# Added quarters of a Strassen product formed in DRAM by accumulating transfers

## The reference

```
o_a, sfa, sba = gdn_branch(qkv, z_a, gate_cols, p, s_af, s_ab)
o_b, sfb, sbb = lru_branch(x_b, z_b, p, s_bf, s_bb, col_major)
pa = o_a @ p['w_proj_a']
pb = o_b @ p['w_proj_b']
g_a, g_b = jnp.split(jax.nn.sigmoid(h @ p['w_gate'] + p['b_gate']), 2, axis=-1)
mixed = (g_a * pa + g_b * pb) @ p['w_out']
return x + gate * mixed, sfa, sba, sfb, sbb
```

## Time and profile before

| | |
|---|---|
| median of 3 runs | 1506.69 us |
| profiled execution | 1505.08 us |
| its span | 1503.2 us |
| PE busy | 1463.1 us, 97% |
| DVE, ACT, POOL busy | 77%, 57%, 32% |
| granted clock, mean | 0.993 |
| DMA queue of SP | 142.12 MB, 30.3% of the 16 engines |

### The profile page before, as it was taken

How to read it: one execution, slowest core, us unless ns; L and a number is a source line. 1 busy time by engine, 2 the same in 40 slices (tenths; PEclk the granted TensorE clock), 3 DMA queues, 4 the chain that set the end, 5 groups by cost and what they waited for, 6 DMA issues and landing times. The chain is left out here.

```text
span 1503.2 us, 29073 instructions
## 1 busy us (share of the span) xinstructions
PE 1463.1 (97%) x11568; PEld 1401.1 (93%) x11568; DVE 1156.2 (77%) x1943; ACT 850.3 (57%) x1789; POOL 478.8 (32%) x376
## 2 busy tenths in 40 slices
PE   8999999999999999999999999999999998897997
PEld 7899999999999999999899999999999898897886
DVE  5789898988889898988847663663666689889864
ACT  6675847576675847575496376376376543443211
POOL 2122323222322323222212221221221686877420
PEclk9999999999999999999999999999999999999999
DMA  9422121222213131323212112112114747436242
GB/s 314 115 71 87 33 90 37 59 69 59 78 35 106 33 97 30 101 73 124 68 52 81 58 51 81 58 51 81 58 51 154 209 139 219 145 122 208 88 154 99
DMA packets 158409, 144.31 MB, mean 96 GB/s; under 512 B 7897, under 2 KB 139842, under 8 KB 158274
## 3 DMA queue, kind: packets, MB, share of 16 engines
q1 hardware_dynamic: 157986, 142.12, 30.3%
q10 hardware_dynamic: 288, 0.33, 0.1%
HBM read 122.34 MB, written 20.09 MB: 95 GB/s over the span
## 5 line engine op out<-in xcount | busy, mean ns | idle before, releaser
L139 PE MATMUL db<-h_hi,w_hi 128*128 128x384 f32 x816 | 288.0, 353 | 0.2 <-DVE w_lo L1477 0.2
L141 PE MATMUL db<-h_hi,w_lo 128*128 128x384 f32 x816 | 274.6, 336 | 0.0
L140 PE MATMUL db<-h_lo,w_hi 128*128 128x384 f32 x816 | 274.6, 336 | 0.0
L140 PE MATMUL mb<-h_lo,w_hi 128*128 128x384 f32 x696 | 233.9, 336 | 0.0
L139 PE MATMUL mb<-h_hi,w_hi 128*128 128x384 f32 x696 | 233.9, 336 | 0.0
L141 PE MATMUL mb<-h_hi,w_lo 128*128 128x384 f32 x696 | 233.9, 336 | 0.0
L2145 POOL TENSOR_TENSOR w_lo<-w,w_hi 128x1024 fp32r<-128x1024 f32 x29 | 81.3, 2805 | 314.3 <-ACT w_hi L2195 314.3
L2443 PE MATMUL mb<-h_hi,w_hi 128*128 128x288 f32 x448 | 138.3, 309 | 22.7 <-POOL w_lo L2156 22.3
L139 PEld LDWEIGHTS db<-h_hi,w_hi 128*128 128x128 f32 x816 | 153.7, 188 | 3.9 <-DVE w_lo L1477 0.7
L140 PEld LDWEIGHTS db<-h_lo,w_hi 128*128 128x128 f32 x816 | 153.9, 189 | 0.0
L141 PEld LDWEIGHTS db<-h_hi,w_lo 128*128 128x128 f32 x816 | 153.4, 188 | 0.0
(11 more groups left out here) (374 smaller groups left out, 3499.3 us busy)
## 6 DMA issues: line engine op xcount, KB each, us to landing
w<-in_w_in SPq DMA_DIRECT2D x48, 512.0 KB, 4.1
d_dt<-decay_rows SPq DMA_DIRECT2D x16, 576.0 KB, 6.6
d_qg<-decay_rows SPq DMA_DIRECT2D x16, 512.0 KB, 4.2
w<-in_w_gate SPq DMA_DIRECT2D x16, 512.0 KB, 4.2
w<-in_w_proj_a SPq DMA_DIRECT2D x24, 256.0 KB, 3.8
m_w<-in_w_proj_a SPq DMA_DIRECT2D x24, 256.0 KB, 3.4
w<-in_w_proj_b SPq DMA_DIRECT2D x24, 256.0 KB, 3.3
m_w<-in_w_proj_b SPq DMA_DIRECT2D x24, 256.0 KB, 3.2
```

The costliest lines, as they stand in the source:

```text
L139: pe.matmul(out, hi, rhi, start=(k == 0), stop=False)
L140: pe.matmul(out, hi, rlo, start=False, stop=False)
L141: return pe.matmul(out, lo, rhi, start=False, stop=(last and stop))
```

## The change

Two new DRAM arrays hold added quarters: `weight_sums` (four sums of 512 x 512 for each branch) and `row_sums` (three sums of 512 x 576 for each branch). Each is made by two transfers from DRAM to DRAM that POOL issues: the first copies one quarter, the second adds another one to it (`accum_op`). Since such a transfer can only add here, the signs of the scheme are chosen so that seven of the ten two-quarter operands are sums; product 6 takes its rows with the sign turned as they are split, and the results of products 1 and 6 are copied and added with other signs.

The weights' sums are formed during the eight heads of the front stage: in head h, POOL issues the adding transfer of sum h-1 and the copying one of sum h behind the low half of that head's second tile. Branch a's row sums follow behind low halves 4 and 8 of the 29 tiles, branch b's behind feeds 4 and 12 of the Strassen stage (about turns 3 and 11). Left to POOL and DVE in the stage are the weight sum of product 1 (phases 1 and 8) and the row sums of products 4 and 3 (phases 4, 5, 11, 12).

Rows are now loaded for each phase by itself, 14 loads in place of 8 (`QUAD` says into which of the four places), each when the low halves of the phase before in that place are done (`quads_in`). Rows are split one turn later than before: part_high(w+7) and part_low(w+6). The transposition of the branch b states in PE's list moves from turn 2 to turn 3.

```diff
+W_SUMS = ((5, (0, 0), (0, 1)), (7, (0, 1), (1, 1)), (2, (1, 0), (1, 1)), (6, (1, 0), (0, 0)))
+R_SUMS = ((1, (0, 0), (1, 1)), (7, (1, 0), (1, 1)), (6, (0, 0), (0, 1)))
+def row_sum(pool, W, src, br, at, second):
+    j, l = R_SUMS[at][1 + second]
+    part = src[j * KH * P:(j + 1) * KH * P, l * TH:(l + 1) * TH]
+    if second:
+        pool.dma_start(W.rsums[br, at], part, accum_op=ALU.add).then_inc(W.sems["dram_sums"], 16)
+    else:
+        pool.dma_start(W.rsums[br, at], part).then_inc(W.sems["dram_sums"], 16)
...
                 low(block_of(h, 1))
+                if h:
+                    pool.wait_ge(S["dram_sums"], 16 * (2 * h - 1))
+                    weight_sum(pool, A, W, h - 1, 1)
+                weight_sum(pool, A, W, h, 0)
                 pool.wait_ge(S["bf"], (h + 1) * Q)
...
-        COPIES = {5: ((0, 1, 1.0), (0, 0, -1.0)), 1: ((1, 1, 1.0),), 2: ((1, 0, 1.0),)}
+        COPIES = {5: ((0, 1, 1.0), (0, 0, -1.0)), 1: ((1, 1, -1.0),), 2: ((1, 0, 1.0),)}
...
+        QUAD = (0, 1, 2, 1, 2, 3, 1, 2, 0, 3, 1, 0, 3, 1)
+        WITH = {4: 1, 5: 0, 11: 1, 12: 2}
...
+                if m in R_SUM:
+                    sp.wait_ge(S["dram_sums"], 16 * (28 if br else 22))
+                    part = W.rsums[br, R_SUM[m]]
...
+            def quads_in(after, ns):
+                sp.wait_ge(S["r_lo"], was["r_lo"] + KH * (after + 1))
+                for n in ns:
+                    quad_in(n)
...
+                if m in W_SUM:
+                    sp.dma_start(raw_of(n)[:, 0:KH, :], W.wsums[br, W_SUM[m]].rearrange("(k p) n -> p k n", p=P)[
+                        :, :, p * P:(p + 1) * P]).then_inc(S[raw_sem(n)], 16)
+                    return
...
+                if n == 8:
+                    quads_in(1, (3,))
+                elif n == 12:
+                    quads_in(2, (4,))
+                elif n == 20:
+                    quads_in(4, (6, 7))
+                elif n == 24:
+                    quads_in(5, (8, 9))
...
+                if n == 4:
+                    pool.wait_ge(S["dram_sums"], 16 * 22)
+                    pool.wait_ge(S["store"], was["store"] + 16 * H)
+                    for at in range(len(R_SUMS)):
+                        row_sum(pool, W, ob, 1, at, 0)
+                elif n == 12:
+                    pool.wait_ge(S["dram_sums"], 16 * 25)
+                    for at in range(len(R_SUMS)):
+                        row_sum(pool, W, ob, 1, at, 1)
...
-                if w + 2 * KH < NPH * KH:
-                    part_high(w + 2 * KH)
+                if w + 2 * KH <= NPH * KH:
+                    part_high(w + 2 * KH - 1)
```

More of the change, by code:

```diff
@@ L1957, in tail_stage @@
         part_sums = lambda n, j: R.xt[:, n % 4 * 2 + j // 2, j % 2 * TH:(j % 2 + 1) * TH]
-        n_rsums = lambda n: KH * sum(R_PARTS[m][1] is not None for _, m in phases[:n])
+        n_rsums = lambda n: KH * sum(i in WITH for i in range(n))
         acc_of = lambda p, i, l, s: acc[:, p, i, l * TH + s * SW:l * TH + (s + 1) * SW]
@@ L2044, in gate_in @@
                 elif k < 3:
-                    sp.wait_ge(S["r_sum"], was["r_sum"] + n_rsums(NPH - 2))
+                    sp.wait_ge(S["r_lo"], was["r_lo"] + KH * (NPH - 1))
                 else:
@@ L2219, in part_high @@
                 n, j = divmod(q, KH)
-                br, m = phases[n]
-                parts, op = R_PARTS[m]
-                if op is not None:
+                if n in WITH:
                     act.wait_ge(S["r_sum"], was["r_sum"] + n_rsums(n) + j + 1)
@@ L2327, in tail_scalar @@
                         feed_high(0)
-                        for q in range(2 * KH):
+                        for q in range(2 * KH - 1):
                             if q == KH:
@@ L2572, in part_sum @@
                 n, j = divmod(q, KH)
-                br, m = phases[n]
-                parts, op = R_PARTS[m]
-                if op is None:
+                if n not in WITH:
                     return
                 if j == 0:
-                    for part in parts:
-                        dve.wait_ge(S[f"r_in{quad_n[part]}"], quad_count(part, br))
+                    dve.wait_ge(S[f"r_in{QUAD[n]}"], quad_count(n))
                 wait_part(dve, n, j)
-                dve.tensor_tensor(part_sums(n, j), quads[parts[0]][:, j, :], quads[parts[1]][:, j, :], op
+                dve.tensor_tensor(part_sums(n, j), quads[QUAD[n]][:, j, :], quads[WITH[n]][:, j, :], ALU.subtract
                                   ).then_inc(S["r_sum"], 1)
@@ L2585, in part_low @@
                 n, j = divmod(q, KH)
-                parts, op = R_PARTS[phases[n][1]]
                 dve.wait_ge(S["r_hi"], was["r_hi"] + q + 1)
-                dve.tensor_tensor(part_lo(n, j), quads[parts[0]][:, j, :] if op is None else part_sums(n, j),
-                                  part_hi(n, j).bitcast(F32), ALU.subtract).then_inc(S["r_lo"], 1)
+                hi = part_hi(n, j).bitcast(F32)
+                if phases[n][1] == 6:
+                    ins = dve.scalar_tensor_tensor(out=part_lo(n, j), in0=quads[QUAD[n]][:, j, :], scalar=-1.0, in1=hi,
+                                                   op0=ALU.mult, op1=ALU.subtract)
+                else:
+                    ins = dve.tensor_tensor(part_lo(n, j), part_sums(n, j) if n in WITH else quads[QUAD[n]][:, j, :], hi,
+                                            ALU.subtract)
+                ins.then_inc(S["r_lo"], 1)
             def add_up(w):
```

134 lines of the change are left out of this document (77 added, 57 removed).

## The result

The changed kernel takes 1509.63 us (median of 20 runs, 1507.68 to 1512.70) against 1505.90 of the kernel before beside it: ratio 1.0025, 95% interval 1.0018 to 1.0032. It is slower by 3.7 us, 0.25%, where I had forecast 28 us faster. The profiled execution took 1512.44 us with a span of 1510.4, near the upper end of the 20.

A forecast was written before the change was run, and what follows sets the result against it. TensorE, 97% busy, was taken as the bound, losing 37.3 us above the Strassen stage's floor to operand preparation; 1505.08 less 37.3 plus 9 us of new costs gave 1476.8, 1478.4 as median, 8-in-10 range 1468 to 1506.

The forecast's parts named there:

- POOL's transfers in the stage: Strassen stage, branch b's row sums: POOL's issues at 1.3 us each cost 3 us; bounds nothing and 16.
- The front: Later projections: branch a's row sums stand between low halves of whole tiles, where POOL waits for ACT; cost nothing.
- The rule of the Trainium skill: POOL-issued transfers take about 2.0 us plus bytes over 436 GB/s without holding POOL; forecast 3 us lower.
- Phase 0, phases 6 and 7, phases 10 to 13: Strassen stage: losses of 5.3, 12.6 and 11.7 us (phases 12 and 13) go, leaving 0, 1 and 1 us.
- The end chain: Stage end: DVE's branch b folds finish late, delaying output tile 7's low half; 1 us left, bounds 0 and 4.
- Contention: Stage: bursts of row-sum transfers and row loads fill the DMA engines, delaying weight loads; 2 us, bounds 0 and 10.
- The heads: Eight front-stage heads: weight-sum transfers meet SP's load and may delay DVE's solve; 2 us, bounds 0 and 35.
- The sum: Whole kernel: 1505.08 - 37.3 + 3 + 2 + 1 + 1 + 2 = 1476.8 us; with 1.6 for the runs' median, 1478.4.
- A: Stage and heads: accumulating transfers three to four times a plain load hold up SP and weight loads; 1514 us, chance 0.19.
- B: Stage: POOL held by each issue, DVE and POOL obstruct each other; four gaps of 4 us, 1494 us, chance 0.19.
- C: Stage: the wait only moves; row parts a turn late at 8 places return 26 us; 1503 us, chance 0.06.

The follow-up runs named there:

- e1: Changed kernel with branch b's six row-sum transfers spread, one each behind feeds 4, 7, 11, 14, 18 and 21; 1480.34 us, ratio 0.9831.
- e2: Changed kernel with both branches' row-sum transfers spread one by one, in the stage and the projections; 1471.66 us, ratio 0.9775 (run again: 1472.57 us).
- e6: Changed kernel, bursts kept, plus four small POOL copies that nobody reads, behind projections 14, 17, 20 and 23; 1500.63 us, ratio 0.9967.
- e5: e2 with the weight sums taken back to POOL, two quarters loaded, no transfers in the heads; 1492.27 us, ratio 0.9909.
- p1: Probe: changed kernel with the heads' weight-sum transfers replaced by bursts of one transfer pattern per head, sums not formed; 1505.36 us, one execution.

## Why the prediction was wrong

- **POOL's transfers in the stage (3 us): the step that failed.** It took 1.3 us an issue, with the upper bound "POOL held for a whole landing each", 16 us for the first burst. The first burst cost 14.3 us (phases 0 and 1), close to the upper bound, the second 15.1 (phases 2 and 3), and I had priced that one at nothing by not naming it. Stage: 29.4 us instead of 3. The mistake was to choose a price per issue near that of SP, which is another queue, and to take it times three. A single issue is even cheaper, 0.65 us (1.04 accumulating); what costs is the hold of the next one until all in flight have landed, 6 to 11 us in the stage. The state of the queue that a burst meets has no row in before, so the far bound had to weigh on every burst, the second and the front's too. With the bursts spread (e1, e2) the term is 0.
- **The front (nothing).** "Where POOL waits for ACT" covers an issue, not a hold of 11.8 + 9.1 us: POOL's low halves there are 9 to 18 us apart. It cost 6.5 us from one matmul's start to the next (6.3 of them idle) and 2.5 of slow matmuls behind it.
- **The rule of the Trainium skill** (DMA: Bandwidth & Descriptors, Anatomy of one DMA) would have made the term of POOL's transfers 0. It holds for one transfer: POOL goes on after 0.65 us. It says nothing of a second behind it; the traces decide.
- **Phase 0, phases 6 and 7, phases 10 to 13 (all but 2 us of 37.3 go).** Right: in e2 the stage takes 178.4 us against the floor of 178.5, with granted clock 1.00. VectorE in phases 6 and 7 keeps PE's pace of 3.19 us a turn, where I had counted 4.0 and left 1 us for the lag; none is left (after, in the folds of branch a):

```profile
1296.03 0.81 DVE L2675 TENSOR_TENSOR m_acc<-m_acc,mb 128x288 f32<-128x288 f32 x2
1296.76 1.27 DVE L2659 TENSOR_TENSOR h_lo<-m_rows,h_hi 128x576 fp32r<-128x576 f32 x1
1297.95 1.35 DVE L2679 SCALAR_TENSOR_TENSOR mixed<-mixed,m_acc 128x1152 f32<-128x1152 f32 x1
```

- **The end chain (1 us, bounds 0 and 4).** Under-sized: in e2 PE waits 3.6 us behind the stage, and the piece behind it is 4.1 us longer than in before, the upper bound. It shows not at output tile 7, where I looked, but at the first ones, because the low halves of the rows queue behind the fold of tile 3 in VectorE's order. In before that fold ended at 1388.8, 5.3 us ahead of PE; in after it ends when the stage does, 1397.4 (VectorE):

```profile
1393.39 2.63 DVE L2686 SCALAR_TENSOR_TENSOR m_gate<-m_gate,m_acc 128x1152 f32<-128x1152 f32 x1
1396.06 1.36 DVE L2689 TENSOR_TENSOR mixed<-mixed,m_gate 128x1152 f32<-128x1152 f32 x1
...
1398.07 1.35 DVE L2638 TENSOR_TENSOR h_lo<-mixed,h_hi 128x1152 fp32r<-128x1152 f32 x1
```

- **Contention (2 us).** None in e2, where the engines' share reaches 1.10 and loads land after up to 10 us without PE waiting. It is 6 us in e6 for one burst that goes out at once, and about 10 in e5, where the transfers are spread but POOL needs twice the loads. The upper bound of 10 was thus no mere caution, but in the changed kernel nothing of it shows beside the holds.
- **The heads (2 us).** The number fits the profiled execution of after, whose matmuls stand 1.6 to 2.5 us later from 310 us on, but that is luck. The same transfers run in the heads of e1, e6 and twice of e2, and there the matmuls stand 0.3, 1.1, 0.3 and 1.3 us later. Two executions of e2 alone differ by 1.0 us there. No run shows a cost of the transfers, and what makes the difference is open.
- **The sum** with measured terms: 1505.1 - 37.3 + 29.4 (stage) + 11.0 (up to the stage, by the table: 9.0 of the front's burst, the rest differs from execution to execution) + 4.2 (behind the stage) = 1512.4, as in the profiled execution; the median of the 20 is 2.8 us lower. Without the 29.4 and the 11.0 it is 1472.0, and e2's profiled execution took 1471.7: 5 us better than the 1476.8 forecast for it.
- **The rivals.** A (accumulation three to four times a plain load) fell: a packet of 2304 bytes takes 196 ns where it is accumulated and 93 as a load, a factor of 2.1 in the DMA engines' time, but a whole accumulating row sum lands in 9.6 us (median), 1.7 times the 5.5 us of a load. The prediction allowed 12 each, and no wait for a sum is among SP's. B named the mechanism, "POOL is held by each issue", and its sign came: POOL idle with its issues between, before the low halves of phases 1 and 3. It sized it at four places in the stage of 4 us each; there are two, of 14 and 15 us, and one in the front that B did not have. Its other half, VectorE and POOL in each other's way, made no gap. C did not occur: from phase 4 on no turn is late.

Not tried: the row parts' later turn by itself, apart from their sums.

## What to carry to other kernels

Transfers that POOL issues are better spread than put in a row: one costs 0.65 to 1.05 us, the next can hold the engine for as long as everything in flight takes. Whether that costs time depends on what the engine would have done meanwhile: nothing in the heads, 38 us of the kernel in the stage and the projections. Where the kernel before shows nothing of an engine's queue, price the burst and not the issue, at the far bound, and in every place where it stands. And split a change in time: the same edit with twelve transfers moved is 2.25% faster than before (e2) where as given it is 0.25% slower.

## What the runs showed of the hardware

- POOL's transfers behave as if they went through lists of limited room, counted in rows: of 512-row copies at most three go out together (p1, e6) and sometimes one (after), of 128-row copies six did, of accumulating ones of 512 rows never two. The fitted lists of 128 entries told 71 issues and then e6's three copies before it ran.
- Other POOL instructions are not held by transfers in flight; only the next transfer is. In after the sum at 1209.85 starts as the issue ends, 5 us before that transfer lands.
- Accumulating 1152 KB takes the DMA engines 2.2 times the time of a copy (512 packets of 2304 bytes at 196 ns, against 256 of 4608 at 178), but it lands only some 1.4 times later: in 9.6 us in the median (9.2 to 12.6), where a lone copy takes 5.7 to 6.9 (after).
- Full DMA engines (share 1.10 over phase 1 of e2) cost PE nothing; three copies set off within 2 us (e6) made POOL wait 7.2 us for a weight load, and in e5 weight quarters beside two row loads and one accumulating transfer landed after 13.1 and 14.5 us.
